# Opening of an expert stage: expert ranking in three parts, counts and gates moved, small rows one tile sooner

## What is computed

```python
def moe_swiglu(x, w_router, w_gate, w_up, w_down):
    logits = (x @ w_router).astype(jnp.float32)
    top_vals, top_idx = lax.top_k(logits, TOP_K)
    top_w = jax.nn.softmax(top_vals, axis=-1)
    gates = jnp.sum(jax.nn.one_hot(top_idx, N_EXPERTS, dtype=jnp.float32) * top_w[..., None], axis=-2)
    out = jnp.zeros_like(x)
    for e in range(N_EXPERTS):
        out = out + gates[..., e:e + 1].astype(x.dtype) * swiglu(x, w_gate[e], w_up[e], w_down[e])
    return out
```

## Time and profile before

| | us |
|---|---|
| median of three runs (lowest, highest) | 1392.83 (1390.17, 1393.66) |
| the profiled execution | 1392.43 |
| its span, first to last instruction | 1390.7 |
| PE busy | 1332.4 (96%) |
| DVE busy | 1147.9 (83%) |
| ACT busy | 990.2 (71%) |
| POOL busy | 96.9 (7%) |
| mean granted TensorE clock | 0.994 |

### The profile page before, as it was taken

The page is one execution under the profiler, slowest core; times in us unless marked ns, Lnnn a source line. Parts: engine busy times, 40 slices in busy tenths (PEclk is TensorE's granted clock), DMA queues, the critical chain, the costliest instruction groups (busy, mean ns, idle before and its releaser), DMA issues.

```text
span 1390.7 us, 19504 instructions
## 1 busy us (share of the span) xinstructions
PE 1332.4 (96%) x6863; PEld 1145.8 (82%) x6863; DVE 1147.9 (83%) x1052; ACT 990.2 (71%) x959; POOL 96.9 (7%) x112
## 2 busy tenths in 40 slices
PE   9999999999999999999999999999999998999987
PEld 8988888888997887878779888788888887787865
DVE  5776554466665898999999999999999999899986
ACT  5555444446555777888978888888888898787884
POOL 2000000000000086300000000000000002000000
PEclk9999999999999999999999999999999999999999
DMA  9657855567542799999999999999999999999980
GB/s 321 238 164 277 287 195 182 182 218 229 181 137 72 284 355 415 409 411 412 391 409 396 411 411 412 400 412 410 410 412 409 402 412 409 411 409 397 397 351 30
DMA packets 137062, 454.51 MB, mean 327 GB/s; under 512 B 8233, under 2 KB 29749, under 8 KB 124718
## 3 DMA queue, kind: packets, MB, share of 16 engines
q1 hardware_dynamic: 130272, 429.95, 80.6%
q0 software_dynamic: 4832, 17.13, 3.4%
q10 hardware_dynamic: 1902, 6.70, 1.4%
HBM read 437.99 MB, written 15.75 MB: 326 GB/s over the span
## 4 chain that ended last, share of the span: by engine, by line
PE 56%; DMA 18%; DVE 13%; issue 7%; ACT 5%; SPq 1%; ACTq 0%; DVEq 0%
PE banks L1228 15%; PE banks L1777 13%; DVE w_lo L2000 10%; DMA raw<-in_o_exp_down 8%; DMA raw<-in_o_exp_gate 7%; PE banks L1262 6%; PE banks L1798 5%; PE banks L1536 4%; PE banks L1850 4%; PE banks L1814 3%; ACT w_hi L684 3%; DMA raw<-in_e_w_in 1%; DMA raw<-in_o_exp_up 1%; PE banks L1761 1%; SPq L394 1%
## 5 line engine op out<-in xcount | busy, mean ns | idle before, releaser
L2000 DVE TENSOR_TENSOR w_lo<-raw,w_hi 128x1792 fp32r<-128x1792 f32 (+1 forms) x454 | 919.6, 2063 | 123.4 <-PE banks L1228 50.0
L684 ACT ACTIVATE w_hi<-raw 128x1792 fp32r<-128x1792 f32 (+1 forms) x454 | 784.1, 1736 | 273.3 <-PE banks L1228 79.7
L1798 PE MATMUL banks<-w_lo,x_hi 128*128 128x448 f32 x512 | 131.5, 379 | 18.7 <-DVE w_lo L2000 18.4
L1798 PEld LDWEIGHTS banks<-w_lo,x_hi 128*128 128x128 f32 x512 | 91.0, 188 | 45.4 <-DVE w_lo L2000 39.5
L1777 PE MATMUL banks<-w_hi,x_hi 128*128 128x448 f32 x512 | 127.5, 371 | 0.0
L1777 PE MATMUL banks<-w_lo,x_hi 128*128 128x448 f32 x512 | 125.1, 366 | 1.8 <-DVE w_lo L2000 1.8
L1798 PE MATMUL banks<-w_hi,x_hi 128*128 128x448 f32 x512 | 125.4, 367 | 0.0
L1777 PE MATMUL banks<-w_hi,x_lo 128*128 128x448 f32 x512 | 124.7, 365 | 0.0
L1228 PE MATMUL banks<-w_hi,x_lo 128*128 128x512 f32 (+1 forms) x304 | 108.5, 357 | 0.3 <-DVE x_lo L2035 0.3
L1228 PE MATMUL banks<-w_hi,x_hi 128*128 128x512 f32 (+1 forms) x304 | 108.1, 356 | 0.0
L1228 PE MATMUL banks<-w_lo,x_hi 128*128 128x512 f32 (+1 forms) x304 | 108.1, 356 | 0.0
(11 more groups left out here) (340 smaller groups left out, 1827.3 us busy)
## 6 DMA issues: line engine op xcount, KB each, us to landing
raw<-in_o_exp_gate SPq DMA_DIRECT2D x128, 896.0 KB, 8.1
raw<-in_o_exp_up SPq DMA_DIRECT2D x128, 896.0 KB, 8.8
raw<-in_o_exp_down SPq DMA_DIRECT2D x96, 1024.0 KB, 8.4
raw<-in_o_exp_down SPq DMA_DIRECT2D x32, 512.0 KB, 7.9
raw<-in_o_w_qkv SPq DMA_DIRECT2D x12, 1024.0 KB, 5.2
raw<-in_e_ffn_gate SPq DMA_DIRECT2D x11, 1024.0 KB, 5.1
raw<-in_e_ffn_up SPq DMA_DIRECT2D x11, 1024.0 KB, 5.3
raw<-in_e_ffn_down SPq DMA_DIRECT2D x11, 1024.0 KB, 5.0
```

The costliest lines, as they stand in the source:

```text
L684: act.activation(w_hi[:, at % HI, 0:size], raw[:, at % RAW, 0:size], ACT.Copy).then_inc(hi_made, 1)
L1798: mm = pe.matmul(bank[first + f][:, 0:CUT // 2], x_two[:, 2 * k + kk, :], w[:, kk, f * (CUT // 2):(f + 1) * (CUT // 2)], start=start and k ...
L2000: ve.tensor_tensor(w_lo[:, at % LO, 0:size], raw[:, at % RAW, 0:size], w_hi[:, at % HI, 0:size], ALU.subtract)\
```

## The change

On DVE, `rank_counts` is cut into three functions: the comparison of counts (`rank_counts`), ranks and 0/1 matrices (`rank_experts`), and ids, small positions and `pick_s` (`name_experts`). The first stands behind the split of tile 6, the second behind that of tile 7, the third behind that of tile 8. `share_routes` is cut in two: `count_pairs` (number of pairs, `count_ready`) stands behind tile 10's split, the gates (`share_routes`) behind tile 17's. The clears of banks 4 and 5 move from behind tile 16 to behind tile 22. On PE `gather_small` comes after tile 8, on ACT `gathered_small` one `st` sooner. In the last block ACT's `up_copy` moves ahead of the split of tile 22.

```diff
@@ final_half (ACT)
-                for i in range(16, 19):
+                for i in range(16, 18):
                     st(i, j, b, True)
                 used(19, j, b)
                 up_copy()
+                split_at(18 + HI, j, b, True)
                 split_at(19 + HI, j, b, True)
@@ opening (ACT)
                 st(8, None, None)
+                gathered_small()
                 st(9, None, None)
-                gathered_small()
@@ PE
                 wide_up(2, k, 8 + k, None, None)
-                if k == 1:
+                if k == 0:
                     gather_small()
@@ DVE
                 link(ve.tensor_tensor(more, more, same, ALU.add))
+            def rank_experts():
                 link(ve.tensor_reduce(erank[:, 1:], more, AX, ALU.add))
...
                 link(ve.tensor_tensor(small_terms, pos1[:, :, 1:], by_rank[:, WIDE_RANKS].unsqueeze(1).broadcast_to((P, TT, O)), ALU.mult))
+            def name_experts():
                 ve.tensor_reduce(ids, rank_ids, AX, ALU.add)
...
-            def share_routes():
+            def count_pairs():
...
                 ve.tensor_scalar(job_int[:, LAST_AT:LAST_AT + 1], extras[0:1], float(DUOS - 1), None, ALU.add).then_inc(count_ready, 1)
+            def share_routes():
                 ve.wait_ge(gates_made, 1)
...
             split(OUT1_T + 3 + LO)
+            split(PROJ1_T + LO)
             rank_counts()
-            split(PROJ1_T + LO)
-            for i in range(4, 9):
-                lo(i)
+            lo(4)
+            rank_experts()
+            lo(5)
+            name_experts()
+            lo(6)
+            lo(7)
+            count_pairs()
+            lo(8)
             gathered_small()
             lo(9)
             lo(10)
             hidden_wide(None, None)
             lo(11)
-            share_routes()
             lo(12)
             lo(13)
+            low_wide(None, None)
+            lo(14)
+            share_routes()
+            for i in range(15, 20):
+                lo(i)
             for half in range(2):
                 ve.memset(bank[4 + half], 0.0).then_inc(small_cleared, 1)
-            low_wide(None, None)
-            for i in range(14, 24):
+            for i in range(20, 24):
                 lo(i)
```

## The result

Six executions of the changed kernel have a median of **1385.90 us** (1383.78 to 1387.53), six of the kernel before 1393.24 (1390.17 to 1395.88). The ratio is 0.995 (0.9934 to 0.9966): 7.0 us less, faster by more than the 0.3% of the prediction. The profiled execution took 1387.05 us, with a span of 1385.3.

A forecast was written before the change was run, and what follows sets the result against it. The stream of weight transfers was taken as the bound, so the opening wins by running it earlier. Opening 3.4 plus end 0.5 gave 3.9 us: 1392.43 to 1388.5 profiled, 1388.9 with the median's 0.4; range 1386.5 to 1392.5.

The forecast's parts named there:

- The opening: Tiles 4 to 23, ahead of the loop: PE's path and the weight stream each gain 3.4 us; bounds 1.4 and 5.4.
- the slow start of 316 GB/s: Weight transfers after the empty queue: tiles 13 to 15 take 8.7 us at this rate, counted once.
- the long-run rate for the other 11.93 MB: Weight stream after tile 15, up to tile 28: 409 GB/s, 29.2 us, so tile 28 lands at 507.0.
- A: Whole kernel, the forecast itself: one slow start, then the long-run rate; 1388.9 us, chance 0.42.
- C: Opening's stream: both slow stretches stay, being a matter of the tiles; gain 1.4 + 0.5, 1390.9 us, chance 0.15.
- The price of the ids: SP's load 12 waits for the later ids, leaving 4.0 us later at 464.3; DMA engines idle for these 4 us.
- D: Opening's stream: late ids win, backlog drains below 355 GB/s; tile 28 lands 5.2 us late, 1397.5 us, chance 0.07.
- GpSimd: Its row arithmetic starts and ends some 5 us later, at no cost; cover 80 us before the loop's fourth step.
- The end: Last block: copy of up sums first, first turn 1.5 us sooner, second limits gain to 0.5 us; bounds 0 and 1.5.
- Rival E: Whole kernel: no effect on the time, PE ahead anyway or rate near break-even; about 1392.3 us, chance 0.06.
- the 0.4 of the median: Whole kernel: the profiled execution, 1392.43 us, lay 0.40 below the median 1392.83; added to 1388.5 to forecast the median.
- B: Opening's stream: 409 GB/s from the start, gain 5.4 + 0.5; 1386.9 us, chance 0.30.

The follow-up runs named there:

- gates_old: The changed kernel with gates and clears back at their old places on DVE, the count of pairs staying behind tile 10's split; ratio 0.9976 to the kernel before.
- in_gaps: The changed kernel with the ranking's first two pieces in DVE's waits round the wide rows, ids behind the split of tile 6; 1385.10 us, 0.9943 of before.
- a_again: The changed kernel run once more, unedited, beside new runs of the kernel before; 1386.74 us, ratio 0.9973.
- in_gaps_2: The changed kernel with the ranking in DVE's waits round the wide rows, the same kernel as in_gaps, run again in another set; 1383.57 us, 0.9959 of before.

## Why the prediction was right and wrong

*The opening: right.* Load 12 was forecast at 464.3, landed at 469.1, ACT's copy to end at 472.5, DVE's rows to begin at 472.6, PE at 486.4; they were 464.40, 469.3, 472.70, 472.73 and 486.35. Tile 15 came 8.1 us behind tile 12 where the slow start of 316 GB/s made it 8.7. Tile 28 was forecast at 507.0 and landed at 507.5: there "the long-run rate for the other 11.93 MB" was a little high, because 494 to 500 stayed at 356 GB/s. So the stream went between A and C, close to A. Over profiles, tile 28 landed 2.9 us sooner (61.9 against 59.0, means of three and four), `m_lo` 3.2 sooner; forecast 3.4 for both. At the second gate copy, near 540, the lead is 7.9, because the scatter of the rows, which takes bytes from the stream (last section), lies ahead of this copy in the kernel before and behind it in the changed one (in gates_old, with the early scatter, the lead there is 1.5); at the third it is 3.6, at the 13th 3.9: it is carried, as "from about 493 us on the stream is never dry again" has it.

*The price of the ids: right in kind.* The 4 us of idle DMA engines are real (254 GB/s in 464 to 470) and outweighed; D is refuted by 416 GB/s in the row behind it. The debt was paid in 476 to 494, though, and not at once. And I did not weigh the price as avoidable: in_gaps shows 3.2 us more to be had there.

*GpSimd: the size wrong, the cover right.* Forecast 5 us later, measured 10.7 in this profile, with 75 us left to the fourth step's loads, and 21 in another (a_again), with 64 left. The prediction let the arithmetic last as long as before; it lasted 5.7 us longer, and its first part, up to the row numbers, 17 us longer. In the time that cost nothing that a mark shows.

*The end: in kind as forecast.* The wait moved from the first turn to the second; its 0.5 us is what the marks average, and the ratios don't resolve it.

*The Trainium skill's HBM figure.* By the estimate from *DMA: Bandwidth & Descriptors* in the Trainium skill (Specifications, about 358 GB/s for one core, given as half of a stack's 716; here one core ran alone) tile 28 would have landed at 510.1 and the gain been 0.8 us. The trace disagrees: 412 GB/s in 504 to 524 and 409 over 200 us, and tile 28 at 507.5. Rival E, near the same time, is out with it: 0.9973 in each of two sets, with intervals below 0.9985.

*The number: wrong, at the step "with the 0.4 of the median, 1388.9 us", and in the range at "B with a little scatter".* The sum itself, 3.9 us, is borne out by two sets of 12 runs: 3.8 us each, with intervals from 2.2 to 5.3. What I took as known is the level that it is subtracted from, and how near a measured median would come to it. The median of three runs, 1392.83, stood for the kernel's time to within 0.4 us. But single executions scatter by about 2 us, and larger sets of the same kernel have medians of 1391.23, 1392.79 and 1391.23; with the first and the last of these as the level the same sum gives 1387.3, and there the changed kernel had 1386.74 and 1386.82, inside my range. Of the 3.0 us by which 1385.90 lies below the forecast, that arithmetic puts 1.6 on the level, 0.5 on a gain somewhat above the sum, and 0.9 on a median of six that came out below those of 12.

This doesn't explain the first comparison by itself. Its own six runs of before have 1393.24, above my level and not below it, and its gain of 7.0 us (4.7 to 9.2) is larger than the sum. As far as is known that is the scatter of two medians of six: up to the 13th gate copy its profile agrees with the later ones. A part of it may be the dip near 1260, which the earlier stream met less often. Why this set came out so far apart stays open. The range had the fault that it left 0.4 us below B for all this. With the 2 us of an execution it would have begun near 1385 and held the result. The same holds for the chance of faster: I split it by the mechanisms, and gave the measurement's own scatter no part of it. That "faster" came true in the first comparison was luck by the same measure: in both later sets the ratio was 0.9973, less than 0.3%.

## What to carry to other kernels

Where transfers bound a loop and none of its queues runs dry, an opening is worth about the lead that its stream has when it first saturates (here 2.9 us at tile 28 and 3.9 at the 13th gate copy; for in_gaps 6.2 and 7.2); follow one named tile's landing and one mark late in the loop, both counted from the last event ahead of the change. Small vector work that others wait for belongs in the idle stretches that the timeline shows for its engine (here 1.49 and 0.88 us ahead of the wide rows), and not merely behind the next split: a work item that releases a queue of loads is late for all of them. Before forecasting a gain of 0.3%, ask how well the level is known: three runs that scatter by 2 us give it to a few us only.

## What the hardware showed that I had not expected

- The time ahead of any edit differs by up to 3.4 us between executions of kernels alike up to there (446.88 to 450.31 at the load of tile 10).
- A saturated stream of 409 GB/s has single dips of some 4 us to 306 to 362 GB/s near 1260 us, in some executions and not in others of the same kernel (in_gaps 354 in 1256 to 1260, in_gaps_2 417); the three steps round them take 1.7 us longer on average (168.1 against 166.4), with overlap.
- GpSimd's scatter of 2.1 MB of rows takes half of the DMA engines' bytes while it lasts. Queues in 544 to 552 of the changed kernel, q0 the scatter and q1 the weights (packets, MB, share of 16 engines):

```profile
q0 software_dynamic: 466, 1.71, 52.3%
q1 hardware_dynamic: 473, 1.63, 50.1%
```

The sum stays at 418 GB/s, so the windows don't show it: the weights get 204 GB/s, and PE is partly idle from 548 on, where in the kernel before the same scatter lay in 516 to 535.
- TensorE's granted clock no longer falls at 484 to 490. Instead it falls between 553 and 559 in most of the changed kernels' profiles, behind that stretch in which PE was partly idle (in gates_old, whose scatter is early, at 541); in_gaps_2:

```profile
552.00:556.00 4.00, 2.39 (x8) 1.86 (x9) 3.15 (x2) 2.88 (x3) 3.84 (x6) 0.70 1.02 407
556.00:560.00 4.00, 4.00 (x12) 3.58 (x11) 3.44 (x3) 3.61 (x4) 3.92 (x5) 0.50 1.05 414
```

The DMA engines go on at 407 and 414 GB/s through it; whether it costs anything no run shows.
